# Three 256-column projection passes become one of 512 and one of 256, with the halves added by VectorE

## The chip, the cores and the metric

One core of one Trainium2 chip. The time is that of one execution of the whole program on the device, in microseconds (us); less is better. TensorE does the matrix products (a weight load and a matmul for each), ScalarE (ACT in the profile) the activations and conversions, VectorE (DVE) the elementwise arithmetic, and SyncE (SP) issues the transfers from HBM. A product leaves TensorE in a PSUM bank; the other two engines read it from there.

## The reference

The model is three layers over 256 tokens of width 1024. The change lies in the second half of the first layer, a mixture of 16,384 experts. Cut to what is computed there:

```python
u = expert_down[experts]                       # the chosen experts' input rows
act = gelu(einsum('cd,chkd->chk', xc, u))      # each expert's own projection of the token
w = gates * act
return einsum('chk,chkd->cd', w, expert_up[experts])
```

The kernel gathers nothing. It computes the projection of all 256 tokens on every expert, multiplies by a gate that is zero for an expert not chosen, and multiplies the result with all rows of `expert_up`.

## The kernel before

The experts are 128 chunks of 128. A chunk needs its projection (experts x tokens, from `peer_down`), the gelu of it, the gate, and then the product of these weights with the chunk's 128 x 1024 block of `peer_up`, added up over all chunks in four PSUM banks, `experts_acc`.

Products are made exact enough by splitting each fp32 operand into a high part that TensorE's fp32r format holds and a low part, what is left. `three_passes` then does high x high, high x low and low x high into the same PSUM columns (lines 187, 188, 189).

The projections of the first 52 chunks (`READY` is 28 + 24) are done earlier, in plain fp32. Those of the other 76, chunks 52 to 127, are the business of `Projections` and `experts_phase`. `hT` is the activation in its high and low part, each 8 slices (`k`) of 128 x 256 tokens. For chunk n:

- SP loads `down_raw` (in two halves) and then `ffn_h`, the raw rows of `peer_up`, in one queue.
- ACT writes `down_high`, DVE `down_low` (`split_high`, `split_low`, two halves each).
- TensorE does 8 x three passes of 256 columns into the left half of the bank `projection0` or `projection1`.
- ACT applies the gelu from that bank into `experts_full`, of which there is one; DVE multiplies it by the gate (`spread`), and writes its high and low part, `experts_wh` and `experts_wl`.
- ACT and DVE split the rows of `peer_up` into `experts_uh` and `experts_ul`; TensorE does 4 x three passes of 512 columns into `experts_acc`.

Every engine runs its own instructions in the written order and waits on semaphores. On TensorE the projection of chunk n + 1 stands ahead of the sum of chunk n:

```python
def both(n, b):
    proj.project(pe, n + 1, 1 - b)
    add(n, b)
```

ACT's order in a round is `split_high(n + 1)`, gelu of n, split of the rows n. DVE's is `split_low(n + 1)`, the gate of n, the weights of n, the low part of the rows n. The first two rounds and the last two are written out, the rest is a loop of two rounds.

Of the kernel before, what the change touches and what calls it, by code (L numbers as in the profile page):

```python
# [30 lines left out]
P = 128  # L31
# [1114 lines left out]
class Projections:  # L1146
# [3 lines left out]
    def __init__(self, nc, ctx, down, hT, raw):  # L1150
        self.down, self.hT, self.raw = down, hT, raw
        self.high, self.low = [[ctx.enter_context(nc.sbuf_tensor(f"down_{n}{b}", [P, KD, P], F32R)) for b in range(2)]
                               for n in ("high", "low")]
        self.u = [ctx.enter_context(nc.psum_tensor(f"projection{b}", [P, 512], F32)) for b in range(2)]
        self.landed = [[ctx.enter_context(nc.semaphore(f"down_landed{b}_{h}")) for h in range(2)] for b in range(2)]
        self.highs, self.lows, self.projected, self.done = [
            ctx.enter_context(nc.semaphore(n)) for n in ("down_highs", "down_lows", "projected", "gelu_done")]
# [25 lines left out]
    def project(self, pe, n, b):  # L1183
        m = n - READY
        for h in range(2):
            pe.wait_ge(self.lows, m * 2 + (h + 1))
            if h == 0:
                wait(pe, self.done, m - 1)
            for k in range(KD // 2 * h, KD // 2 * (h + 1)):
                mm = three_passes(pe, self.u[b][:, 0:SEQ], [v[b][:, k, :] for v in (self.high, self.low)],  # L1190
                                  [v[:, k, :] for v in self.hT], k == 0, k == KD - 1)
            mm.then_inc(self.projected, 1)

    def gelu(self, act, n, b, into):
        m = n - READY
        act.wait_ge(self.projected, m * 2 + 2)
        act.activation(into, self.u[b][:, 0:SEQ], ACT.Gelu).then_inc(self.done, 1)  # L1197
# [289 lines left out]
def experts_phase(nc, up, early, spread, x, proj, spare):  # L1487


    with ExitStack() as c:  # L1490
# [56 lines left out]
        def _(act):  # L1547
# [6 lines left out]
            def one(n, b):  # L1554
                if not isinstance(n, int) or n + 1 < NKEYS:
                    proj.split_high(act, n + 1, 1 - b)
                wait(act, wgt_ready, n)
                proj.gelu(act, n, b, full[:])
# [11 lines left out]
        def _(dve):  # L1570
# [10 lines left out]
            def one(n, b):  # L1581
                if not isinstance(n, int) or n + 1 < NKEYS:
# [4 lines left out]
                weights(n, b, full[:])  # L1587
            over_chunks(dve, 0, EARLY, lambda n, b: weights(n, b, early[:, n, :]))
            proj.split_low(dve, READY, 0)
            over_chunks(dve, EARLY, READY, lambda n, b: weights(n, b, early[:, n, :]))  # L1590
            for b in range(2):
                one(READY + b, b)
# [29 lines left out]
def build(nc, d, out, upto=99, start=0):  # L1622
    ctx = ExitStack()
    with ctx:
# [7 lines left out]
        hT = [sb(f"hT_{n}", [P, KD, SEQ], F32R) for n in ("high", "low")]  # L1632
# [37 lines left out]
        if start < 2 <= upto:  # L1670
            with ExitStack() as c:
# [18 lines left out]
                proj = Projections(nc, c, d["downT"], hT, plain.raw)  # L1690
# [71 lines left out]
```

## Time and profile before

| | before |
|---|---|
| three runs | 1721.66, 1725.54, 1726.55 us, median 1725.54 |
| profiled execution | 1728.26 us, of which 1726.2 us are the span of its instructions |
| TensorE busy in the span | 1564.6 us (91%) |
| VectorE busy | 1074.9 us (62%) |
| ScalarE busy | 699.1 us (40%) |
| mean granted TensorE clock | 0.955 of full speed |

Matmul records overlap: one of 256 columns shows a duration of 0.28 us where the next starts 0.12 us later. What a pass costs in a full row of passes is the distance from one start to the next. "Idle" in brackets behind a row is the time that the engine sat before it, and whose work ended that.

### The profile page before, as it was taken

Reading aid. Unit: us, or ns where it says so; the run is one execution under the profiler, and the core shown is the slowest. Engines: PE = TensorE matmul, PEld = TensorE weight load, DVE = VectorE, ACT = ScalarE, POOL = GpSimd, SP = SyncE. Lnnn points to the kernel's source line nnn. Section 1 sums busy time; section 2 is a strip of 40 time slices with the busy share of each in tenths; the row PEclk is TensorE's granted clock in tenths of the full one; section 3 lists DMA queues with packets and bytes.
Section 4 is the critical chain, followed back from the end, with each engine's and each line's share of the span. In section 5 each row is a group of like instructions: output and inputs, shape, how many; then the busy total and the mean of one; then the engine's idle time right before and its main releaser. Section 6 shows DMA issues by size and latency. Waiting matters only on the chain. (4 is left out here: it accounts for less than half of the span.)

```text
span 1726.2 us, 28966 instructions
## 1 busy us (share of the span) xinstructions
PE 1564.6 (91%) x8809; PEld 1383.0 (80%) x8809; DVE 1074.9 (62%) x2752; ACT 699.1 (40%) x1526; POOL 5.8 (0%) x13
## 2 busy tenths in 40 slices
PE   2997789998998999999999999879999997869987
PEld 1664578887997888999999999779999997658885
DVE  3577457957997776666666666555555554266663
ACT  0343211113323443544444444346555554336552
POOL 0000000000000000000000000000000000000000
PEclk9998789999999999999999999989999999679997
DMA  6410043442224555555555555374444441075410
GB/s 246 164 38 1 2 160 111 153 153 75 92 90 142 194 191 188 194 184 182 194 184 182 194 184 183 127 261 135 151 152 137 134 139 45 1 250 165 121 26 25
DMA packets 162586, 239.33 MB, mean 139 GB/s; under 512 B 41808, under 2 KB 91472, under 8 KB 161488
## 3 DMA queue, kind: packets, MB, share of 16 engines
q1 hardware_dynamic: 162160, 238.34, 42.2%
q8 instruction: 37, 0.61, 0.2%
q14 instruction: 37, 0.30, 0.1%
q10 hardware_dynamic: 352, 0.07, 0.0%
HBM read 237.09 MB, written 1.28 MB: 138 GB/s over the span
## 5 line engine op out<-in xcount | busy, mean ns | idle before, releaser
L187 PE MATMUL experts_acc<-experts_uh,experts_wh 128*128 128x512 f32 x512 | 201.5, 394 | 5.7 <-DVE experts_ul L1579 5.7
L188 PE MATMUL experts_acc<-experts_ul,experts_wh 128*128 128x512 f32 x512 | 201.1, 393 | 0.0
L189 PE MATMUL experts_acc<-experts_uh,experts_wl 128*128 128x512 f32 x512 | 200.1, 391 | 0.0
L1132 PE MATMUL plain_u<-ffn_h,down_raw 128*128 128x256 f32 x832 | 192.1, 382 | 0.4 <-PEq L1217 0.4
L1552 ACT ACTIVATE experts_uh<-ffn_h 128x512 fp32r<-128x512 f32 x256 | 147.1, 624 | 83.7 <-PE experts_acc L189 79.1
L189 PE MATMUL projection<-hT_high,down_low 128*128 128x256 f32 x608 | 172.1, 283 | 0.0
L188 PE MATMUL projection<-hT_low,down_high 128*128 128x256 f32 x608 | 172.0, 283 | 0.0
L187 PE MATMUL projection<-hT_high,down_high 128*128 128x256 f32 x608 | 171.7, 282 | 0.0
L1132 PEld LDWEIGHTS plain_u<-ffn_h,down_raw 128*128 128x128 f32 x832 | 154.1, 192 | 19.5 <-issue 1.1
L1579 DVE TENSOR_TENSOR experts_ul<-ffn_h,experts_uh 128x512 fp32r<-128x512 f32 x256 | 164.7, 684 | 3.0 <-ACT experts_uh L1552 3.0
L187 PE MATMUL mix_a_pj<-mix_a_wh,hT_high 128*128 128x384 f32 x384 | 136.8, 356 | 17.0 <-DVE mix_a_wl L560 17.0
L188 PE MATMUL mix_a_pj<-mix_a_wl,hT_high 128*128 128x384 f32 x384 | 130.1, 339 | 0.0
L189 PE MATMUL mix_a_pj<-mix_a_wh,hT_low 128*128 128x384 f32 x384 | 130.0, 339 | 0.0
L1585 DVE TENSOR_TENSOR experts_full<-experts_full,spread 128x256 f32<-128x256 f32 x76 | 32.3, 426 | 143.1 <-ACT experts_full L1197 143.1
L187 PEld LDWEIGHTS projection<-hT_high,down_high 128*128 128x128 f32 x608 | 116.4, 191 | 2.9
L188 PEld LDWEIGHTS projection<-hT_low,down_high 128*128 128x128 f32 x608 | 116.4, 191 | 2.9
L187 PEld LDWEIGHTS experts_acc<-experts_uh,experts_wh 128*128 128x128 f32 x512 | 97.1, 190 | 24.4 <-issue 6.1
L189 PEld LDWEIGHTS projection<-hT_high,down_low 128*128 128x128 f32 x608 | 116.4, 191 | 0.0
L189 PEld LDWEIGHTS experts_acc<-experts_uh,experts_wl 128*128 128x128 f32 x512 | 96.7, 189 | 20.8
L1173 ACT ACTIVATE down_high<-down_raw 128x512 fp32r<-128x512 f32 x152 | 95.0, 632 | 40.9 <-DMA down_raw<-in_downT 34.8
L188 PEld LDWEIGHTS experts_acc<-experts_ul,experts_wh 128*128 128x128 f32 x512 | 97.1, 190 | 17.4
L560 DVE TENSOR_TENSOR mix_a_wl<-mix_a_w_raw,mix_a_wh 128x1536 fp32r<-128x1536 f32 (+1 forms) x64 | 93.6, 1489 | 19.5 <-ACT mix_a_wh L710 16.3
(274 smaller groups left out, 3014.9 us busy)
## 6 DMA issues: line engine op xcount, KB each, us to landing
down_raw<-in_downT SPq DMA_DIRECT2D x256, 256.0 KB, 3.4
ffn_h<-in_up SPq DMA_DIRECT2D x256, 256.0 KB, 2.8
mix_a_w_raw<-in_wa SPq DMA_DIRECT2D x48, 768.0 KB, 5.9
block_w_raw<-in_w SPq DMA_DIRECT2D x16, 768.0 KB, 6.6
mix_b_w_raw<-in_wb SPq DMA_DIRECT2D x16, 768.0 KB, 6.7
route_raw<-in_route SPq DMA_DIRECT2D x16, 576.0 KB, 3.7
wo<-in_wo SPq DMA_DIRECT2D x2, 2048.0 KB, 10.4
mix_a_w_raw<-in_wa SPq DMA_DIRECT2D x16, 256.0 KB, 3.3
```

The lines of the kernel that those rows point to most:

```text
L187: pe.matmul(out, lhs[0], rhs[0], start=start, stop=False, skip_group_check=True)
L188: pe.matmul(out, lhs[0], rhs[1], start=False, stop=False, skip_group_check=True)
L189: return pe.matmul(out, lhs[1], rhs[0], start=False, stop=stop, skip_group_check=True)
L560: eng.tensor_tensor(wl[w][:, k, c], pieces.raw[w][:, k, c], wh[w][:, k, c].bitcast(F32), ALU.subtract).then_inc(lows, 1)
L1132: mm = pe.matmul(self.u[b][:, 0:SEQ], self.raw[b][:, k, :], self.h[:, k, :], start=k == 0, stop=k == KD - 1, skip_group_check=True)
L1173: act.activation(self.high[b][:, self.half(h)], self.raw[b][:, self.half(h)], ACT.Copy).then_inc(self.highs, 1)
L1552: act.activation(uh[b][:, w], raw_u[b][:, w], ACT.Copy).then_inc(u_high, 1)
L1579: dve.tensor_tensor(ul[b][:, w], raw_u[b][:, w], uh[b][:, w].bitcast(F32), ALU.subtract).then_inc(u_low, 1)
L1585: dve.tensor_tensor(full[:], full[:], spread[:, n - READY, :], ALU.mult)
```

## The change

The two activation parts become one tensor, `hT_both`, so that one matmul can read slice k of both: 256 columns of the high part and 256 of the low part, 8 KB apart. With the high weights loaded once, it writes high x high to the left half of the bank and high x low to the right half. The low weights then meet the high activations as before, into the left half. VectorE adds the halves into `experts_full` (a copy of one, a drain, an addition of the other), and ScalarE applies the gelu there in place. The semaphore `summed` now releases the gelu and the bank. The new step of VectorE for chunk n + 1 stands at the end of its round n, and for the first chunk right before the first round.

```diff
     def project(self, pe, n, b):
         m = n - READY
+        u = self.u[b][:]
         for h in range(2):
             pe.wait_ge(self.lows, m * 2 + (h + 1))
             if h == 0:
-                wait(pe, self.done, m - 1)
+                wait(pe, self.summed, m - 1)
             for k in range(KD // 2 * h, KD // 2 * (h + 1)):
-                mm = three_passes(pe, self.u[b][:, 0:SEQ], [v[b][:, k, :] for v in (self.high, self.low)],
-                                  [v[:, k, :] for v in self.hT], k == 0, k == KD - 1)
+                pe.matmul(u.rearrange("p (a t) -> p a t", a=2), self.high[b][:, k, :], self.hT[:, :, k, :], start=k == 0, stop=False,
+                          skip_group_check=True)
+                mm = pe.matmul(u[:, 0:SEQ], self.low[b][:, k, :], self.hT[:, 0, k, :], start=False, stop=k == KD - 1,
+                               skip_group_check=True)
             mm.then_inc(self.projected, 1)
 
-    def gelu(self, act, n, b, into):
+    def sum_halves(self, dve, n, b, into):
+
         m = n - READY
-        act.wait_ge(self.projected, m * 2 + 2)
-        act.activation(into, self.u[b][:, 0:SEQ], ACT.Gelu).then_inc(self.done, 1)
+        dve.wait_ge(self.projected, m * 2 + 2)
+        dve.tensor_copy(into, self.u[b][:, 0:SEQ])
+        dve.drain()
+        dve.tensor_tensor(into, into, self.u[b][:, SEQ:], ALU.add).then_inc(self.summed, 1)
+
+    def gelu(self, act, n, v):
+        m = n - READY
+        act.wait_ge(self.summed, m + 1)
+        act.activation(v, v, ACT.Gelu).then_inc(self.done, 1)
...
                 proj.split_high(act, n + 1, 1 - b)
-                wait(act, wgt_ready, n)
-                proj.gelu(act, n, b, full[:])
+                proj.gelu(act, n, full[:])
...
             def one(n, b):
-                if not isinstance(n, int) or n + 1 < NKEYS:
+                more = not isinstance(n, int) or n + 1 < NKEYS
+                if more:
                     proj.split_low(dve, n + 1, 1 - b)
                 dve.wait_ge(proj.done, n - (READY - 1))
                 dve.tensor_tensor(full[:], full[:], spread[:, n - READY, :], ALU.mult)
                 dve.drain()
                 weights(n, b, full[:])
+                if more:
+                    dve.drain()
+                    proj.sum_halves(dve, n + 1, 1 - b, full[:])
...
+            proj.sum_halves(dve, READY, 0, full[:])
             for b in range(2):
                 one(READY + b, b)
...
-        hT = [sb(f"hT_{n}", [P, KD, SEQ], F32R) for n in ("high", "low")]
+        hT_both = sb("hT", [P, 2, KD, SEQ], F32R)
+        hT = [hT_both[:, n] for n in range(2)]
```

On VectorE, where the first two rounds begin, before (after the loop over the ready chunks):

```order
L1206 COMPARE_AND_BRANCH
L1180 TENSOR_TENSOR down_low<-down_raw,down_high 128x512 x2
L1585 TENSOR_TENSOR experts_full<-experts_full,spread 128x256
L1574 CAST experts_wh<-experts_full 128x256
L1576 TENSOR_TENSOR experts_wl<-experts_full,experts_wh 128x256
L1579 TENSOR_TENSOR experts_ul<-ffn_h,experts_uh 128x512 x2
```

The same place now:

```order
L1217 COMPARE_AND_BRANCH
L1201 COPY experts_full<-projection 128x256
L1203 TENSOR_TENSOR experts_full<-experts_full,projection 128x256
L1180 TENSOR_TENSOR down_low<-down_raw,down_high 128x512 x2
L1596 TENSOR_TENSOR experts_full<-experts_full,spread 128x256
L1584 CAST experts_wh<-experts_full 128x256
L1586 TENSOR_TENSOR experts_wl<-experts_full,experts_wh 128x256
L1589 TENSOR_TENSOR experts_ul<-ffn_h,experts_uh 128x512 x2
L1201 COPY experts_full<-projection 128x256
L1203 TENSOR_TENSOR experts_full<-experts_full,projection 128x256
```

Two instructions that read the finished projection (`projection`) have come in ahead of the next chunk's low weights (`down_low`), at the start and in each round.

On TensorE, the end of a loop's sum and the first products of the next projection, before:

```order
L189 MATMUL experts_acc<-experts_uh,experts_wl 128x512
L1206 REGISTER_ALU
L1206 COMPARE_AND_BRANCH
L187 MATMUL projection<-hT_high,down_high 128x256
L188 MATMUL projection<-hT_low,down_high 128x256
L189 MATMUL projection<-hT_high,down_low 128x256
```

A piece of a projection now, inside the loop:

```order
L1187 ISA
L1191 MATMUL projection<-hT,down_high 128x512
L1193 MATMUL projection<-hT,down_low 128x256
L1191 MATMUL projection<-hT,down_high 128x512
L1193 MATMUL projection<-hT,down_low 128x256
```

Three matmuls for a slice k, of 768 columns together, have become two, of 768 columns together.

## Rows read from the trace of the kernel before

**Rows 1.** Stretch, length, busy us (xinstructions) of PE, PEld, DVE, ACT, POOL; PEclk, DMA, GB/s.
```profile
692.62:1108.50 415.88, 415.88 (x2666) 379.55 (x2665) 263.62 (x519) 196.94 (x368) 0.00 (x0) 1.00 0.56 185
```

**Rows 2.** Waits, 692.62 to 1108.50 us: engine line <- releaser, us, times, longest.
```profile
ACT experts_full L1197 <- PE projection L189: 174.2, 73, 2.9
DVE experts_full L1585 <- ACT experts_full L1197: 134.5, 72, 1.9
```

**Rows 3.** Timeline of TensorE: start us, us, engine line op.
```profile
692.62 0.40 PE L187 MATMUL experts_acc<-experts_uh,experts_wh 128*128 128x512 f32 x1
...
1002.65 0.39 PE L188 MATMUL experts_acc<-experts_ul,experts_wh 128*128 128x512 f32 x1
...
1004.24 0.39 PE L189 MATMUL experts_acc<-experts_uh,experts_wl 128*128 128x512 f32 x1
1004.47 0.28 PE L187 MATMUL projection<-hT_high,down_high 128*128 128x256 f32 x1
1004.58 0.28 PE L188 MATMUL projection<-hT_low,down_high 128*128 128x256 f32 x1
...
1007.22 0.28 PE L189 MATMUL projection<-hT_high,down_low 128*128 128x256 f32 x1
1007.34 0.40 PE L187 MATMUL experts_acc<-experts_uh,experts_wh 128*128 128x512 f32 x1
```

**Rows 4.** Timeline of TensorE in the next layer, passes of 384 columns.
```profile
1251.78 0.34 PE L187 MATMUL mix_a_pj<-mix_a_wh,hT_high 128*128 128x384 f32 x1
...
1255.25 0.34 PE L189 MATMUL mix_a_pj<-mix_a_wh,hT_low 128*128 128x384 f32 x1
```

**Rows 5.** Timeline of VectorE, its first two rounds.
```profile
683.67 1.28 DVE L1180 TENSOR_TENSOR down_low<-down_raw,down_high 128x512 fp32r<-128x512 f32 x2
690.42 0.43 DVE L1585 TENSOR_TENSOR experts_full<-experts_full,spread 128x256 f32<-128x256 f32 x1 [5.47 <-ACT experts_full L1197]
690.92 0.29 DVE L1574 CAST experts_wh<-experts_full 128x256 fp32r<-128x256 f32 x1
691.29 0.43 DVE L1576 TENSOR_TENSOR experts_wl<-experts_full,experts_wh 128x256 fp32r<-128x256 f32 x1
691.63 1.29 DVE L1579 TENSOR_TENSOR experts_ul<-ffn_h,experts_uh 128x512 fp32r<-128x512 f32 x2
692.84 1.28 DVE L1180 TENSOR_TENSOR down_low<-down_raw,down_high 128x512 fp32r<-128x512 f32 x2
694.04 0.42 DVE L1585 TENSOR_TENSOR experts_full<-experts_full,spread 128x256 f32<-128x256 f32 x1
```

**Rows 6.** VectorE instructions that read PSUM, by group.
```profile
L1439 DVE COPY spread_i<-slots 128x256 f32<-128x256 f32 x2 | 0.8, 420 | 1.0 <-PEq L1217 1.0
L890 DVE TENSOR_TENSOR mix_a_ona<-mix_a_ot,mix_a_inv 128x256 f32<-128x256 f32 x8 | 3.4, 425 | 3.8 <-PE mix_a_ot L662 2.9
```

**Rows 7.** Timeline of ScalarE, the last rounds.
```profile
1099.09 1.31 ACT L1173 ACTIVATE down_high<-down_raw 128x512 fp32r<-128x512 f32 x2 [0.21 <-DMA down_raw<-in_downT]
1108.76 0.39 ACT L1197 ACTIVATE experts_full<-projection 128x256 f32<-128x256 f32 x1 [4.20 <-PE projection L189]
```

**Rows 8.** Timeline of SyncE's queue.
```profile
1004.47 0.93 SPq L1511 DMA_DIRECT2D ffn_h<-in_up  x2
1005.70 0.92 SPq L1163 DMA_DIRECT2D down_raw<-in_downT  x2
```

**Rows 9.** Timeline of TensorE at the second projection and at the last chunks.
```profile
689.74 0.28 PE L187 MATMUL projection<-hT_high,down_high 128*128 128x256 f32 x1
...
1108.50 0.40 PE L187 MATMUL experts_acc<-experts_uh,experts_wh 128*128 128x512 f32 x1
...
1111.25 0.45 PE L187 MATMUL experts_acc<-experts_uh,experts_wh 128*128 128x512 f32 x1
```

**Rows 10.** Timeline of VectorE, the last round.
```profile
1109.18 0.42 DVE L1585 TENSOR_TENSOR experts_full<-experts_full,spread 128x256 f32<-128x256 f32 x1 [3.13 <-ACT experts_full L1197]
1110.39 1.29 DVE L1579 TENSOR_TENSOR experts_ul<-ffn_h,experts_uh 128x512 fp32r<-128x512 f32 x2
```

More of the change, by code:

```diff
@@ L1155, in __init__ @@
         self.landed = [[ctx.enter_context(nc.semaphore(f"down_landed{b}_{h}")) for h in range(2)] for b in range(2)]
-        self.highs, self.lows, self.projected, self.done = [
-            ctx.enter_context(nc.semaphore(n)) for n in ("down_highs", "down_lows", "projected", "gelu_done")]
+        self.highs, self.lows, self.projected, self.summed, self.done = [
+            ctx.enter_context(nc.semaphore(n)) for n in ("down_highs", "down_lows", "projected", "halves_summed", "gelu_done")]
     def load(self, sp, n, b):
@@ L1689, in build @@
                 c1.close()
-                proj = Projections(nc, c, d["downT"], hT, plain.raw)
+                proj = Projections(nc, c, d["downT"], hT_both, plain.raw)
                 experts_phase(nc, d["up"], early, spread, x, proj, plain.h)
```

## The prediction

> **What bounds the kernel now.** I read the busy time of the experts' own stretch first, then its waits, then the timeline of each engine around one round. From the first sum after two projections (692.62 us) to the last but one sum (1108.50) TensorE is busy for all of 415.88 us, at full clock; VectorE for 263.62, ScalarE for 196.94 [rows 1]. That is the proof to look for, and since overlapping matmuls make "busy" flatter TensorE, the waits are the second one: the long waits are ScalarE's for the projection (174.2 us) and VectorE's for the gelu behind it (134.5 us), and TensorE waits for nobody [rows 2]. So in this stretch the end is set by how fast TensorE can start its passes, 74 rounds of 415.88 / 74 = 5.62 us [rows 1, 3]. The round has two parts: the projection, 1004.47 to 1007.34, 2.87 us for 24 passes of 256 columns, and the sum, the other 2.75 us, 12 passes of 512 [rows 3]. The change touches only this stretch of 76 projections and both its ends.
>
> **What a pass costs.** Seven steps from 1002.65 to 1004.24 make 227 ns for a pass of 512 columns, and with the first passes of a sum in, 2.75 / 12 gives 229; I take 228. From 1004.58 to 1007.22 are 22 steps of 256 columns: 120 ns [rows 3]. Passes of 384 columns, 20 steps from 1251.78 to 1255.25, take 173.5 ns [rows 4]. The three lie on one line: 120, 174, 228, that is 54 ns for each 128 columns and 12 ns that every pass pays whatever its width.
>
> **The change on TensorE.** A slice k now has 3 passes of 256, 3 x 120 = 360 ns. Afterwards it has one of 512 and one of 256, 228 + 120 = 348 ns. The number of columns is the same; what goes is one fixed part of 12 ns. Over 8 slices that is 0.096 us in a round, 5.52 in place of 5.62, and over 76 projections (608 slices) 7.3 us.
>
> What the rows don't show is a pass whose 512 columns come from two places 8 KB apart, and passes of two widths in turn. The dear end: the two runs cost what two passes cost, 240 ns, and nothing is saved. The cheap end: the first step of a projection, from a 256 pass that stands behind a 512 one, is 1004.47 to 1004.58, 0.11 us, not 0.12 [rows 3]; if every narrow pass had that, a slice would take 228 + 113 = 341 ns at the best reading of it, and 608 x 19 = 11.6 us would go. A step into the sum, 512 behind 256, shows nothing of such a gain, so I take the value of the long runs, 348.
>
> The Trainium skill ("TensorE: Matmul & The Clock Gate", section "Back-to-back issue gap") gives a warm pass N / 2.4 GHz plus about 2.5 ns, so that a pass less would be worth 2.5 ns and the change 608 x 2.5 = 1.5 us. The trace has 120 ns where that formula has 109, and 228 where it has 216: here the fixed part is some 12 ns, and I go by the trace.
>
> **The change on VectorE, and what hides it.** Each round gets a copy from PSUM, a drain, an addition, and a drain ahead of them. A copy of 128x256 from PSUM takes 0.42 us, an elementwise operation of two operands with one in PSUM 0.425 [rows 6]. Such an instruction, a drain and the next start are 690.42 to 690.92, 0.50 us, and one without a drain ahead of the next 691.29 to 691.63, 0.34 [rows 5]. The first drain is at most the difference, 0.16. A round of VectorE that waits for nothing is 690.42 to 694.04, 3.62 us [rows 5]; it becomes 3.62 + 0.50 + 0.34 + 0.16 = 4.62. TensorE's is 5.52, so VectorE still waits each round, about 0.9 us less what the hand-over costs.
>
> What is queued behind the new wait is the point to check. Let Q be the moment when a projection is through and TensorE begins the sum. ScalarE started on it at Q + 0.26 (1108.50 to 1108.76) [rows 7, 9]; now VectorE does. Copy and addition: the next chunk's low weights start at Q + 0.26 + 0.84 = Q + 1.10 and their first half (1.28 - 0.60 = 0.68 us) is there at Q + 1.8. Before they were made well ahead. TensorE wants them when its sum is through, at Q + 2.75: 1 us to spare. The gelu ends near Q + 1.6, ahead of the low weights' end at Q + 2.3. Then gate 0.50, cast 0.37, subtraction 0.34, first half of the rows' low part 0.68: Q + 4.2, wanted by the sum at Q + 2.75 + 2.78 = Q + 5.5: 1.3 us to spare. SyncE's queue loads the next rows when that low part is done, and the expert weights behind them: before at 1004.47 and 1005.70 [rows 8], which are 2.75 and 3.98 us behind Q = 1001.72 (one round of 5.62 before 1007.34). The first moves to Q + 4.2, 1.5 us later, and the weights with it. ScalarE waited for them until 1099.09, 1.83 us behind its Q of 1108.50 - 2 x 5.62 = 1097.26 [rows 7, 9], so they land at Q + 3.4 now and are converted by Q + 4.7; VectorE takes them at Q + 5.52 + 1.10 = Q + 6.6. All of it is covered. If the cover were gone, each 0.1 us of a round would cost 7.6 us. ScalarE's work is the same; the gelu reads `experts_full` in place of PSUM.
>
> **The two ends, which have no cover.** At the start the low weights of the second projection were made at 683.67, long before, and TensorE went from the first projection into the second at 689.74 without a gap [rows 5, 9]. Now they stand behind the first addition: 689.74 + 0.26 + 0.84 + 0.68 = 691.52. TensorE idles 1.8 us. What follows holds: the rows' low part is there at 691.52 - 0.68 + 1.20 + 1.21 + 0.68 = 693.9, the second projection ends at 691.52 + 2.78 = 694.3. At the end the last sum starts at 1111.25 [rows 9], its rows' first low half being there at 1110.39 + 0.68 = 1111.07 [rows 10], 0.18 us before. Copy, drain and addition push the gelu from Q + 0.26 to Q + 0.26 + 0.50 + 0.43 + 0.04, 0.97 later. The last sum loses 0.97 - 0.18 = 0.8 us. Together 2.6 us.
>
> **The sum.** - 7.3 + 2.6 = - 4.7 us. Made against the profiled execution, 1728.26, it gives 1723.5. That execution lies 2.7 above the median 1725.54 of the three runs, so on the scale of the runs the forecast is 1720.8, 0.27% less. A measurement of this kernel can tell about 0.3% (5.2 us) from no change: the forecast lies just inside that.
>
> **The rivals.**
> A. Nothing is saved on TensorE: the pass that reads two places costs 240 ns. For it speaks that no pass of this trace reads so; against it, that the fixed part is the same at three widths. The time is the two ends alone, + 2.6: 1728.1. (By the formula of the Trainium skill cited above it would be - 1.5 + 2.6 = + 1.1, so 1726.6, between A and the forecast; its page would have A nearly right.)
> B. The narrow pass behind a wide one is cheaper, 341 ns for a slice: - 11.6 + 2.6 = - 9.0, 1716.5. For it speaks the one step of 0.11 us; against it that it occurs once in 24.
> C. Slower: VectorE becomes the bound. Its round of 4.62 and the hand-over of 0.26 make 4.9 us; it decides once the copy, the two drains and the addition cost 0.6 us more than I give them, since the round would then pass 5.52. At a round of 5.8 us the stretch takes 76 x 0.18 = 14 us more than before and the ends 2.6: 1742. Against it: all durations are from rows of the same engine on the same shapes.
>
> **How the numbers follow.** Forecast 0.60, A 0.20, B 0.12, C 0.08. The forecast's own spread is some 3 us to either side, from the runs (1721.66 to 1726.55) and the ends: 1718 to 1724. The range reaches from B, 1716, to A, 1728; C is left out. The forecast falls below 1720.3, that is faster by over 0.3%, in a little under half of its cases (0.27), with B 0.39 in all. Slower by over 0.3% are C and a little of A: 0.09. The rest, 0.52, is within 0.3%.
>
> **What would show it.** In the changed profile: a step from a wide projection pass to the narrow one of 228 ns and back of 120, rounds of 5.52 us, TensorE busy throughout; VectorE waiting for the projection in each round, by 0.6 to 0.9 us; the low weights' first half done 1 us ahead of the projection; one gap on TensorE of 1.8 us ahead of the second projection and one of 0.8 ahead of the last sum. Rounds of 5.62 mean A, of 5.47 B. TensorE waiting for `down_low` or `experts_ul` in every round means C. Wrong it would also be if the clock fell in one of the two gaps, which are short.

## The result, and the profile after

The changed kernel takes 1725.9 us (median of 17 runs, 1723.99 to 1728.99), the kernel before 1717.47 in the runs beside it. The ratio is 1.0045, 95% interval [1.0035, 1.0056]: slower by 0.45%. The forecast was 4.7 us less than before, 1720.8. The profiled execution of the changed kernel has a span of 1722.7 us at a mean clock of 0.959.

The view that splits the span into stretches shows where to look. Its columns are those of [rows 1]. For the changed kernel the cuts are the start of the first projection's first pass and the start of the experts' last pass:

```profile
0.00:686.15 686.15, 610.19 (x2937) 501.55 (x2938) 475.21 (x1492) 192.84 (x519) 1.40 (x7) 0.96 0.36 125
686.15:1113.72 427.57, 425.25 (x2129) 356.90 (x2127) 329.33 (x682) 203.80 (x376) 0.00 (x0) 1.00 0.54 181
1113.72:1722.70 608.98, 523.61 (x3138) 489.12 (x3136) 330.57 (x730) 305.02 (x631) 4.40 (x6) 0.93 0.40 125
```

and the same cuts in the execution profiled before the change was made:

```profile
0.00:686.87 686.87, 611.06 (x2937) 502.16 (x2938) 476.17 (x1494) 192.86 (x519) 1.40 (x7) 0.96 0.37 125
686.87:1113.83 426.96, 426.96 (x2736) 389.55 (x2735) 268.02 (x528) 200.83 (x376) 0.00 (x0) 1.00 0.55 182
1113.83:1726.20 612.37, 526.54 (x3138) 491.27 (x3136) 330.68 (x730) 305.43 (x631) 4.41 (x6) 0.92 0.40 124
```

The changed stage grew by 0.61 us, from 426.96 to 427.57, with a full clock in both. So two questions stand: why the stage didn't shrink by 4.7 us, and where the other 7 us or so of the runs come from. The stretch behind the stage can't answer the second from these two profiles: in the one of before it is the longer, and its clock the lower.

**The first question.** The stretch that answers to [rows 1], from the first sum after two projections to the last but one sum:

```profile
693.62:1107.49 413.87, 413.87 (x2075) 347.79 (x2073) 321.90 (x667) 199.83 (x368) 0.00 (x0) 1.00 0.56 186
```

It is 413.87 / 74 = 5.593 us a round, where the forecast had 5.52 and before had 5.62. The timeline of TensorE in one round (columns as in [rows 3]):

```profile
1001.21 0.40 PE L187 MATMUL experts_acc<-experts_uh,experts_wh 128*128 128x512 f32 x1
1001.46 0.40 PE L188 MATMUL experts_acc<-experts_ul,experts_wh 128*128 128x512 f32 x1
1001.69 0.40 PE L189 MATMUL experts_acc<-experts_uh,experts_wl 128*128 128x512 f32 x1
...
1004.00 0.39 PE L1191 MATMUL projection<-hT,down_high 128*128 128x512 f32 x1
1004.22 0.28 PE L1193 MATMUL projection<-hT,down_low 128*128 128x256 f32 x1
1004.34 0.40 PE L1191 MATMUL projection<-hT,down_high 128*128 128x512 f32 x1
1004.57 0.28 PE L1193 MATMUL projection<-hT,down_low 128*128 128x256 f32 x1
1004.69 0.40 PE L1191 MATMUL projection<-hT,down_high 128*128 128x512 f32 x1
1004.93 0.28 PE L1193 MATMUL projection<-hT,down_low 128*128 128x256 f32 x1
1005.05 0.40 PE L1191 MATMUL projection<-hT,down_high 128*128 128x512 f32 x1
...
1006.81 0.40 PE L187 MATMUL experts_acc<-experts_uh,experts_wh 128*128 128x512 f32 x1
```

The projection is 1004.00 to 1006.81, 2.81 us or 351 ns a slice, forecast 348. The sum is 1001.21 to 1004.00, 2.79 us where it was 2.75; its first step, 1001.21 to 1001.46, is the longest. Both parts are longer than forecast though nobody is waited for. Over 71 rounds a wide pass is followed after 227 to 241 ns, 235 on average, and the narrow one behind it after 113 to 120, 116 on average. So the narrow pass behind a wide one is cheaper, as rival B had it, and the wide one behind a narrow one is dearer by more than that.

The two ends came as forecast. TensorE's timeline at the second projection and at the last sum:

```profile
688.84 0.28 PE L1193 MATMUL projection<-hT,down_low 128*128 128x256 f32 x1
690.74 0.49 PE L1191 MATMUL projection<-hT,down_high 128*128 128x512 f32 x1 [1.61 <-DVE down_low L1180]
...
1110.04 0.39 PE L189 MATMUL experts_acc<-experts_uh,experts_wl 128*128 128x512 f32 x1
1111.13 0.47 PE L187 MATMUL experts_acc<-experts_uh,experts_wh 128*128 128x512 f32 x1 [0.70 <-DVE experts_ul L1589]
```

A pass of 256 is followed by the next after 0.12 us, here after 1.90: 1.78 lost. A pass of 512 is followed after 0.23, here after 1.09: 0.86 lost.

VectorE's waits are what [rows 2] become (686 to 1108 us):

```profile
ACT experts_full L1208 <- DVE experts_full L1203: 134.5, 75, 7.0
ACT down_high L1173 <- DMA down_raw<-in_downT: 79.7, 73, 1.5
DVE experts_full L1201 <- PE projection L1193: 74.6, 75, 6.1
PE projection L1191 <- DVE down_low L1180: 1.6, 1, 1.6
```

VectorE waits for the projection in each of 75 rounds, 6.1 us ahead of the first and (74.6 - 6.1) / 74 = 0.93 in the others; TensorE waits once for VectorE here. ScalarE's wait for the expert weights is the later transfer that the forecast worked out, and nobody waits for it in turn.

### The profile page after: what moved, and what is told of

Its sections match the earlier page's. It is cut to its first block and busy times, and to the rows that moved or that the text cites. A ratio compares the mean times of both kernels' runs of the same rounds, so it can differ in the third digit from the quotient of the medians.

```text
span 1722.7 us, 27941 instructions
## 1 busy us (share of the span) xinstructions
PE 1559.1 (90%) x8201; PEld 1347.6 (78%) x8201; DVE 1135.1 (66%) x2904; ACT 701.7 (41%) x1526; POOL 5.8 (0%) x13
## 5 line engine op out<-in xcount | busy, mean ns | idle before, releaser
L1191 PE MATMUL projection<-hT,down_high 128*128 128x512 f32 x608 | 217.1, 397 | 1.6 <-DVE down_low L1180 1.6
L1193 PE MATMUL projection<-hT,down_low 128*128 128x256 f32 x608 | 170.5, 280 | 0.0
L187 PE MATMUL mix_a_pj<-mix_a_wh,hT 128*128 128x384 f32 x384 | 136.6, 356 | 16.2 <-DVE mix_a_wl L560 16.2
L1191 PEld LDWEIGHTS projection<-hT,down_high 128*128 128x128 f32 x608 | 114.2, 188 | 29.2 <-DVE down_low L1180 1.9
L189 PE MATMUL mix_a_pj<-mix_a_wh,hT 128*128 128x384 f32 x384 | 130.0, 338 | 0.0
L188 PE MATMUL mix_a_pj<-mix_a_wl,hT 128*128 128x384 f32 x384 | 129.9, 338 | 0.0
L1193 PEld LDWEIGHTS projection<-hT,down_low 128*128 128x128 f32 x608 | 114.7, 189 | 2.9
L189 PEld LDWEIGHTS experts_acc<-experts_uh,experts_wl 128*128 128x128 f32 x512 | 96.6, 189 | 22.9
L560 DVE TENSOR_TENSOR mix_a_wl<-mix_a_w_raw,mix_a_wh 128x1536 fp32r<-128x1536 f32 (+1 forms) x64 | 93.8, 1489 | 19.9 <-ACT mix_a_wh L710 16.6
L1180 DVE TENSOR_TENSOR down_low<-down_raw,down_high 128x512 fp32r<-128x512 f32 x152 | 98.1, 686 | 4.5 <-issue 0.3
L597 PE MATMUL block_pj<-block_w_raw,block_h 128*128 128x384 f32 x256 | 91.1, 487 | 1.1 <-PEq L206 1.1
L1208 ACT ACTIVATE experts_full<-experts_full 128x256 f32<-128x256 f32 x76 | 31.8, 418 | 138.6 <-DVE experts_full L1203 138.6
```

Of the source, the lines that this page charges most:

```text
L187: pe.matmul(out, lhs[0], rhs[0], start=start, stop=False, skip_group_check=True)
L188: pe.matmul(out, lhs[0], rhs[1], start=False, stop=False, skip_group_check=True)
L189: return pe.matmul(out, lhs[1], rhs[0], start=False, stop=stop, skip_group_check=True)
L560: eng.tensor_tensor(wl[w][:, k, c], pieces.raw[w][:, k, c], wh[w][:, k, c].bitcast(F32), ALU.subtract).then_inc(lows, 1)
L597: mm = pe.matmul(dst[:, 0:3 * P], hT[:, k, chunks[i][1] * P:(chunks[i][1] + 1) * P], pieces.raw[b][:, k, :], start=k == 0, stop=k == KD - ...
L1180: eng.tensor_tensor(self.low[b][:, k], self.raw[b][:, k], self.high[b][:, k].bitcast(F32), ALU.subtract).then_inc(self.lows, 1)
```

## The experiments

All were timed beside the kernel before on the same chip. "Stage" is the distance between the two cuts above in the kernel's own profile; the last column is the median of the mean granted clocks of its runs. In the runs of before beside them it was 0.963 or 0.964, in those of the changed kernel 0.959 and, the second time, 0.957.

| kernel | median us | ratio [95%] | stage | clock |
|---|---|---|---|---|
| before_again | 1720.93 | 1.0000 [0.9981, 1.0019] | 426.96 | 0.964 |
| after_again | 1728.95 | 1.0041 [1.0024, 1.0059] | 427.64 | 0.957 |
| one_run | 1726.72 | 1.0034 [1.0017, 1.0052] | 427.56 | 0.959 |
| early_low | 1722.11 | 1.0007 [0.9989, 1.0024] | 426.68 | 0.962 |
| before_late | 1719.69 | 0.9999 [0.9986, 1.0012] | 426.97 | 0.964 |
| after_late | 1723.62 | 1.0017 [1.0002, 1.0031] | 427.64 | 0.962 |
| grouped | 1725.37 | 1.0021 [1.0007, 1.0034] | 424.17 | 0.958 |
| narrow_sum | 1726.94 | 1.0034 [1.0023, 1.0046] | 429.77 | 0.961 |
| after_060 | 1726.05 | 1.0048 [1.0035, 1.0062] | 427.61 | 0.960 |
| before_300 | 1720.59 | 1.0015 [1.0005, 1.0025] | 426.93 | 0.963 |
| before_341 | 1719.20 | 1.0010 [0.9999, 1.0021] | 426.96 | 0.964 |
| wide_first | 1721.26 | 1.0017 [1.0006, 1.0027] | 421.36 | 0.960 |
| after_padded | 1722.27 | 1.0031 [1.0020, 1.0042] | 427.58 | 0.964 |
| before_padded | 1723.93 | 1.0037 [1.0023, 1.0051] | 426.93 | 0.962 |
| wide_first_padded | 1716.52 | 0.9990 [0.9977, 1.0002] | 421.37 | 0.963 |
| after_free | 1721.88 | 1.0005 [0.9994, 1.0016] | 427.65 | 0.961 |
| wide_first_free | 1714.32 | 0.9964 [0.9951, 0.9977] | 421.36 | 0.963 |
| before_free | 1720.81 | 1.0024 [1.0015, 1.0033] | 426.96 | 0.961 |

### Is the difference there again, and where

The kernel before and the changed kernel, run again as they are.

> The kernel before, unchanged, for a second profile. The changed stage (first projection to the last sum) took 436.2 us in the profile of before and 436.8 after, while the medians lie 8.4 us apart. Theory T1: the stage is as in the first profile, 436.2 us within 0.3, and the rest of the program is some 9 us shorter than in that profile, because TensorE is granted the low clock for fewer microseconds in the layers behind the stage (it was low for 154 us in the first profile, 140 after); mean clock 0.96 or above. Theory T2: the stage itself is some 8 us shorter than in the first profile (428), which was an odd execution, and the rest is as it was.

> The changed kernel, unchanged. Both theories: a stage of 436.8 us within 0.3, a ratio of 1.003 to 1.006 to before. T1: the later layers take as long as in the first profile of it; T2 says nothing of them.

(The stages of 436.2 and 436.8 us in these texts run on to the next norm's transposes; the cuts of the table end 9.2 us earlier.) The difference came again, 1.0041, and so did the stages, 426.96 and 427.64. The kernel before now showed this stretch behind the stage:

```profile
1115.00:1717.10 602.10, 516.41 (x3138) 482.41 (x3136) 330.89 (x730) 305.33 (x631) 4.41 (x6) 0.95 0.41 126
```

602.10 us at a clock of 0.95, against 612.37 at 0.92 in its first profile: the same instructions, 10 us apart from one execution to the next. In the changed kernel it was 608.98 and 610.0. So what the change costs beside 0.6 us lies behind the changed code, in the two layers that the diff doesn't touch, and single profiles can't be set against each other there.

### The stage: does the pass pay for its two places

The activation as `[slice, part, token]`, so that a wide pass reads one run of 512 columns (the matmuls, cut here, index it to match).

```diff
-        hT_both = sb("hT", [P, 2, KD, SEQ], F32R)
-        hT = [hT_both[:, n] for n in range(2)]
+        hT_both = sb("hT", [P, KD, 2, SEQ], F32R)
+        hT = [hT_both[:, :, n, :] for n in range(2)]
...
```

> The changed kernel with the high and low activations of a slice side by side, so that the wide pass reads one run of 512 columns and not two of 256 that lie 8 KB apart. In the changed kernel a wide projection pass is followed after 227 to 241 ns, mean 235, where 228 were forecast. Theory R (the second run costs time): the step falls to 228, a projection from 2.81 to 2.75 us, the stage by 75 x 0.06 = 4.5 us. Theory S (it is the alternation of wide and narrow passes, whatever is read): steps, round and stage as in the changed kernel, within 0.5 us of the stage. The whole may move differently by the clock of the later layers, if T1 holds.

Projection 2.8101 us, sum 2.7832, stage 427.56: as in the changed kernel. Two places cost nothing. What rival A was built on isn't there.

### The stage: the changes of width

Four wide passes, then four narrow ones, in each half.

```diff
-            for k in range(KD // 2 * h, KD // 2 * (h + 1)):
+            part = range(KD // 2 * h, KD // 2 * (h + 1))
+            for k in part:
                 pe.matmul(u.rearrange("p (a t) -> p a t", a=2), self.high[b][:, k, :], self.hT[:, :, k, :], ...
+            for k in part:
                 mm = pe.matmul(u[:, 0:SEQ], self.low[b][:, k, :], self.hT[:, 0, k, :], ...
```

> The changed kernel, with the passes of a half of a projection grouped: four wide ones, then four narrow ones, in place of wide and narrow in turn. In the changed kernel a projection takes 2.810 us (2.784 forecast) and the sum behind it 2.783 (2.748 before). If it is the change of width that costs (theory S), there are 3 changes in a projection and not 15: projection 2.79 us, sum back near 2.75, round 5.54, stage shorter by 75 x 0.05 = 4 us. If the sum's passes are slow because a wide pass stands right before, or because VectorE reads the bank in that time, nothing changes there.

And all eight wide passes first, which need only the high weights; the low weights' wait then stands behind them. The wide pass and the wait for `summed` go out of the loop (lines cut here).

```diff
+        pe.wait_ge(self.highs, m * 2 + 2)
+        wait(pe, self.summed, m - 1)
+        for k in range(KD):
+            pe.matmul(u.rearrange("p (a t) -> p a t", a=2), self.high[b][:, k, :], self.hT[:, :, k, :], ...
         for h in range(2):
             pe.wait_ge(self.lows, m * 2 + (h + 1))
...
```

> The changed kernel with all eight wide passes of a projection ahead of all eight narrow ones; the wide ones wait only for the high weights, so that TensorE has 1.8 us of work while VectorE makes the low weights of the second projection. In the grouped kernel (three changes of width) projection and sum took 2.780 and 2.767 us, in the changed one (fifteen) 2.810 and 2.783, and with narrow passes alone 2.873 and 2.747. Theory S: with one change of width 2.77 and 2.76, round 5.53 against 5.62 before and 5.593 changed; the gap of 1.85 us goes; stage 426.96 - 75 x 0.09 + 0.9 = 421.1 us, 5.9 below before. Rival: the slow passes behind a wide one cost the same wherever they stand, round 5.55 as grouped, stage 422.6. The whole: 1720 - 5.9 plus what the clock does, 0 to 8.

The projection took 2.780 us with four groups and 2.766 with two; the sum 2.767 and 2.7475, the latter its length of before. The stage fell to 424.17 and 421.36, 3.4 and 6.2 us below the changed kernel's where 4 and 6.5 were expected. The whole did not follow: 1.0021 and 1.0017, still slower than before though the stages are 2.8 and 5.6 us shorter than there. One round with two groups (timeline of TensorE in wide_first_free, whose stage is the same; a row with x8 is eight passes):

```profile
1002.01 1.98 PE L1191 MATMUL projection<-hT,down_high 128*128 128x512 f32 x8
1003.82 1.11 PE L1196 MATMUL projection<-hT,down_low 128*128 128x256 f32 x8
1004.78 0.40 PE L187 MATMUL experts_acc<-experts_uh,experts_wh 128*128 128x512 f32 x1
1005.01 0.40 PE L188 MATMUL experts_acc<-experts_ul,experts_wh 128*128 128x512 f32 x1
```

Eight wide passes in 1.81 us, 226 ns each; eight narrow ones in 0.96, 120 each. That is the 346 ns a slice that the forecast's fixed part asks for (348). Removing a pass does save 13 ns: (2.872 - 2.766) / 8. Fifteen changes of width in a projection, in place of one, give back 5 ns a slice and slow the sum behind it by 36 ns. Two groups leave a gap at the start, but it has moved to the first sum, whose rows' low part is the last thing that VectorE makes there:

```profile
695.96 0.47 PE L187 MATMUL experts_acc<-experts_uh,experts_wh 128*128 128x512 f32 x1 [1.15 <-DVE experts_ul L1594]
```

The first two projections and this gap take 688.92 to 695.96, 7.04 us, where the changed kernel takes 686.15 to 693.62, 7.47.

### The stage: do VectorE's reads of PSUM slow TensorE

High x high and high x low as two passes of 256 again, into the two halves, with VectorE adding as in the changed kernel.

```diff
-                pe.matmul(u.rearrange("p (a t) -> p a t", a=2), self.high[b][:, k, :], self.hT[:, :, k, :], start=k == 0, ...
+                pe.matmul(u[:, 0:SEQ], self.high[b][:, k, :], self.hT[:, 0, k, :], start=k == 0, stop=False, ...
+                pe.matmul(u[:, SEQ:], self.high[b][:, k, :], self.hT[:, 1, k, :], start=False, stop=False, ...
```

> The changed kernel, but the wide pass is two passes of 256 again, high x low into the right half of the bank; VectorE still adds the halves. It does only that half of the change. If the passes of TensorE make the sum slower (theory S), projection 2.872 and sum 2.748 us as before, round 5.62, stage 427 + 1.85 + 0.9 = 429.7 us. If VectorE's two new reads of PSUM beside the sum make it slower (theory V), the sum is 2.783.

Projection 2.8726 and sum 2.7473, both as before. VectorE's copies and additions cost TensorE nothing in a round. The stage is 429.77, which is before's plus 2.8: the two ends alone, and what rival A would have been.

### The stage: the gap at the start

The low weights of the second projection ahead of the first addition (in the first round they are then left out; that line is cut here).

```diff
...
+            proj.split_low(dve, READY + 1, 1)
             proj.sum_halves(dve, READY, 0, full[:])
```

> The changed kernel, but VectorE makes the low weights of the second projection before it adds the halves of the first. The gap of 1.85 us on TensorE ahead of the second projection goes, and nothing else in the stage changes: stage 436.8 - 1.8 = 435.0 us, 1.2 below before. If the stage decided the whole (T2), the whole is 1.8 us shorter than the changed kernel. T1: the whole moves by 1.8 or by another amount, since the stage now ends 1.8 us earlier against the windows of the clock.

The stage lost 0.96 us, not 1.8, and the timeline says why: the gap has moved to the first sum, whose rows' low part is late now.

```profile
693.81 0.47 PE L187 MATMUL experts_acc<-experts_uh,experts_wh 128*128 128x512 f32 x1 [0.66 <-DVE experts_ul L1589]
```

### Behind the stage: is it the moment at which the layers begin

The layers behind the stage have stretches at a granted clock below 1, and a shift in time could place them otherwise. These kernels delay them by idle subtractions of VectorE behind the last sum (results unused): before_late by 0.6 us, before_300 by 3.06, before_341 by 3.46; after_060 by 0.6 and after_late by 2.8. T1 and T1b in the texts below say that the moment at which the later layers begin decides the whole; T0 and the plain theory say that it doesn't. The lines are those of before_300.

```diff
+            for i in range(4):
+                dve.tensor_tensor(ul[0][:, halves[0]], raw_u[0][:, halves[0]], uh[0][:, halves[0]].bitcast(F32), ALU.subtract)
+                dve.drain()
```

> The kernel before, with one idle subtraction of 128x512 on VectorE (0.60 to 0.68 us) between the last sum and what follows it. It puts the end of the stage where the changed kernel has it, 0.6 us later than before, and changes nothing else. Clock theory T1 (the windows in which the low clock is granted lie fixed against the stage, which starts after such a window, and the small shift of its end decides how many windows of the later layers are at the low clock): the whole is 5 to 9 us slower than before, mean clock 0.959 or less, as the changed kernel. Plain theory: it costs its 0.65 us, ratio 1.000 to 1.001.

> The changed kernel, with 2.8 us of idle subtractions on VectorE between the last sum and what follows it. [...] T1: the later layers meet the windows as in before, so the whole is that of before plus some 3.4 us, 1723.6, and FASTER than the changed kernel (1728.9 in the last comparison) although it does 2.8 us more. Plain theory: 2.8 us slower than the changed kernel.

> The changed kernel with 0.6 us of idle work on VectorE between the last sum and what follows. [...] Theory T1b, that this shift decides: here it is +0.2, so 0 or -1, and the whole is 1720.1 + 0.65 + 0.6 - 0.5 = 1721, some 7 us FASTER than the changed kernel though it does 0.6 us more. Theory T0, that the changed program makes the later layers slower by itself: 0.6 slower than the changed kernel, 1727 to 1729.5.

> The kernel before with 3.06 us of idle work at the same place. [...] T1b: + 3.06 + 8 = 11 us slower than before, about 1731, ratio 1.006. T0: + 3.06, ratio 1.0018.

> [...] T1b: +3.44, about 1723.6, ratio 1.002, and so faster by 7 us than the one with 3.06 us. T0: 0.4 us slower than that one.

No delay made the kernel before as slow as the changed one: 0.9999, 1.0015 and 1.0010, and 3.06 and 3.46 us of added work are 0.18% and 0.20%. after_060 stayed at 1.0048. Only after_late fits the theory: with 2.8 us more to do it ran at 1.0017. One in five isn't a cause, and I dropped it for the difference as a whole, though the moment plays a part in after_late that I can't name.

### Behind the stage: where TensorE's code lies

Then I set the later layers of all profiles side by side. One wait differed in every kernel with the changed TensorE program and in none with the length of before (narrow_sum included). It is VectorE's, for the bias tile, behind the last norm: 9.1 to 9.8 us there, 6.7 to 7.5 in the others. For before_again, beginning with the last norm's transposes (`norm_pt`):

```profile
1517.86 3.68 PE L243 MATMUL norm_pt<-ident,norm_h 128*128 128x128 f32 x16 [5.88 <-DVE norm_h L254]
...
1538.22 0.56 DVE L819 TENSOR_TENSOR bias_btile<-bias_braw,near 128x384 f32<-128x384 f32 x1 [7.09 <-DMA bias_braw<-bias_pad]
...
1543.94 0.66 PE L623 MATMUL mix_b_xp<-ident,mix_b_qk 128*128 128x128 f32 x4 [2.20 <-DVE mix_b_qk L813]
```

and for the changed kernel:

```profile
1519.42 3.68 PE L243 MATMUL norm_pt<-ident,norm_h 128*128 128x128 f32 x16 [5.87 <-DVE norm_h L254]
...
1542.21 0.56 DVE L819 TENSOR_TENSOR bias_btile<-bias_braw,near 128x384 f32<-128x384 f32 x1 [9.51 <-DMA bias_braw<-bias_pad]
...
1548.28 1.12 PE L623 MATMUL mix_b_xp<-ident,mix_b_qk 128*128 128x128 f32 x4 [4.97 <-DVE mix_b_qk L813]
```

From the transposes to the tile are 20.36 us in the one and 22.79 in the other, 2.4 more; to TensorE's `mix_b_xp` it is 2.8 more. The other 0.36 us goes with the change on VectorE: from the tile to `mix_b_xp` are 6.1 us in every kernel that adds the halves, narrow_sum too, and 5.7 in those that don't. The view of the transfers has a queue of the kind "instruction" (packets, MB, share); I take its packets for pieces of an engine's own program. In the changed kernel one lands between 1534 and 1536 us, in the middle of the transfer waited for:

```profile
q1 hardware_dynamic: 55, 0.90, 106.5%
q8 instruction: 1, 0.02, 3.0%
```

It is so in all profiles: the eight kernels with the short TensorE program have such a piece of 16 KB between the transposes and the tile, and the twelve others, the later ones with drains among them, have none. But early_low and after_late are among the eight, with waits of 9.2 and 9.1 us and ratios of 1.0007 and 1.0017, so this wait alone doesn't make a kernel slow.

The six written-out projections of the changed kernel have 8 matmuls and 8 weight loads less each. So all code of TensorE behind the stage lies 96 instructions nearer to its start, and by theory F its pieces are fetched at other moments. To test it, 96 drains on TensorE put the code back. First all of them stood behind the last sum:

```diff
             add(NKEYS - 1, 1, stop=True)
+            for _ in range(96):
+                pe.drain()
```

> The changed kernel with 96 drains on TensorE behind the last sum of the experts, where TensorE waits some 9 us anyway. The changed kernel has 96 instructions fewer on TensorE ahead of the later layers than the kernel before (six written-out projections, each with 8 matmuls and 8 weight loads less), so its later code lies 96 instructions nearer to the start; the drains put it back. Theory F (what costs 8 us behind the stage is where TensorE's code lies, since its blocks of code are fetched at other moments): bias_btile starts 17 us behind the last norm_pt matmul instead of 19 to 20, the first mix_b_xp matmul 22.5 to 23.2 behind it instead of 25.2 to 25.9, the mix_a products take 321 us instead of 320, and the whole comes to that of the kernel before plus the stage's 0.65: ratio 1.000 to 1.001. Rival K (the clock or VectorE's program decides, not TensorE's code): bias_btile stays at 19 to 20, ratio 1.004 to 1.005.

> The kernel before with the same 96 drains in the same place, so that its later code lies 96 instructions further from the start than anywhere so far. Theory F: the fetches of TensorE's code in the later layers come earlier in the program's work than in the kernel before, and some of the later steps move: mix_a products above 321 us, or bias_btile at another distance from the last norm_pt than 17 us; in which direction the total goes it does not say. Rival K: nothing behind the stage changes, bias_btile at 16.8 to 17.5, ratio 1.000 within 0.1%.

> Eight wide passes, then eight narrow ones (as in wide_first), with the 96 drains behind the last sum. Its stage was 5.6 us shorter than before's, yet the whole 1.0017. Theory F: with the later code where the kernel before has it, the layers behind take what they take there, so the whole comes to 1720 - 5.6 = 1714.5, ratio 0.996 to 0.997, faster than both kernels. Rival K: it stays at 1.0017.

The later layers came back as theory F said: in after_padded `bias_btile` starts 16.8 us behind the last transpose (19.1 to 19.9 in the unpadded ones), `mix_b_xp` 22.9, mix_a's products take 321.0 us. But the drains took time, some 0.07 us each (an estimate, since no view shows them: from the end of the last sum's last pass to the next norm's first step are 8.3 us, of which 1.4 pass after the last engine is through, as in the changed kernel, and 6.9 / 96 = 0.07), and a barrier of all engines stands behind them, so that the way from the last sum to mix_a's first product grew from 19.3 to 23.7 us. With this 4.4 taken off, the ratios of 1.0031 and 0.9990 would be 1.0005 and 0.9964. The totals that I had put down for after_padded and wide_first_padded failed by this cost. before_padded came out as neither theory had it: theory F named products above 321 us or a moved tile, and they took 319.3 us with the tile at 17.0; rival K named no change within 0.1%, and without the drains' time (here 4.5 us) it is 1.0011.

So in the next three 28 drains stood there and 68 ahead of the transposes of the norm behind it, where TensorE waits 8.8 us in all.

> The changed kernel with the 96 drains where they hold nobody up: 28 behind the last sum of the experts, 68 ahead of the next norm's transposes, each 0.068 us. In after_padded all 96 stood ahead of a barrier and made the stretch from the last sum to mix_a's products 4.4 us longer; taken off, it was 0.2 us above the kernel before. Theory F: that stretch takes 19.3 us again, mix_a's products 321 us, bias_btile 17 us behind the last norm_pt, and the whole is the kernel before plus 0.65 us: ratio 1.000 to 1.001. Rival K (the later layers took their time back only because the drains delayed them): 1.004 or more.

> Eight wide passes, then eight narrow ones, with the drains placed as in after_free. Theory F: the whole is the kernel before less the 5.6 us of the stage: ratio 0.9965 to 0.9975, faster than both. Rival K: 1.001 or more, as in wide_first.

> The kernel before with the same drains in the same two places as in after_free. It asks whether the drains in themselves, and not the position of the code behind them, made after_free quicker by 0.4%. Theory F: the drains give nothing by themselves; the kernel before is moved 96 instructions away from its position and gets 0 to 0.2% slower (before_padded, less the 4.4 us that its drains cost, was 1.9 us slower): ratio 1.000 to 1.002. Rival D (drains in TensorE's idle time keep it, or its clock, in a better state): ratio 0.995 to 0.997, as much below the kernel before as after_free is below the changed kernel.

after_free: 1.0005, where the changed kernel has 1.0045, and 1.0041 on the chip of this run; its interval meets neither of theirs. Its stage is the changed kernel's, 427.65 us, slow steps and gaps and all. wide_first_free: 0.9964 [0.9951, 0.9977], faster than both kernels. In before_free the same drains made the kernel slower, 1.0024, so drains as such give nothing (rival D); it is 0.04% above the range that I gave theory F. There the drains move the code away from where it was. The timeline of after_free:

```profile
1519.50 3.68 PE L245 MATMUL norm_pt<-ident,norm_h 128*128 128x128 f32 x16 [5.88 <-DVE norm_h L256]
...
1539.78 0.56 DVE L821 TENSOR_TENSOR bias_btile<-bias_braw,near 128x384 f32<-128x384 f32 x1 [7.00 <-DMA bias_braw<-bias_pad]
...
1545.86 0.66 PE L625 MATMUL mix_b_xp<-ident,mix_b_qk 128*128 128x128 f32 x4 [2.44 <-DVE mix_b_qk L815]
```

20.28 us from the transposes to the tile. Between 1520 and 1545 us no piece of code is fetched in it; one is between 1514 and 1516, when the transfers have hardly begun.

The products of the layer ahead, mix_a, move as well, with the code in before's place (before_again, after_free) and out of it (before_free, the changed kernel). In the order before_again, before_free, changed kernel, after_free (duration in ns least/median/most, then the first and the last start in us):

```profile
L187 PE MATMUL mix_a_pj<-mix_a_wh,hT_high x384: 334/334/686, 1134.3 to 1454.6; 128*128 128x384 f32 x192
```
```profile
L187 PE MATMUL mix_a_pj<-mix_a_wh,hT_high x384: 334/334/689, 1132.2 to 1451.4; 128*128 128x384 f32 x192
```
```profile
L187 PE MATMUL mix_a_pj<-mix_a_wh,hT x384: 334/334/689, 1133.0 to 1452.5; 128*128 128x384 f32 x192
```
```profile
L187 PE MATMUL mix_a_pj<-mix_a_wh,hT x384: 333/334/687, 1133.4 to 1454.7; 128*128 128x384 f32 x192
```

320.3, 319.2, 319.5 and 321.3 us: here the moved code is 1 to 2 us quicker. Moved code isn't slower everywhere; its place is worth a microsecond or two here, with the other sign than at the bias tile.

What is left of every ratio when its own stage and its added idle time are taken off says how far theory F carries. Put back by drains (four kernels): -0.03 to +0.02%. With before's length: -0.10 to 0% in four, but +0.18% in narrow_sum. Short, as in the changed kernel: +0.30 to +0.50% in six of eight, but +0.09% in early_low and -0.03% in after_late. Longer than before: +0.11% in before_padded, +0.23% in before_free.

## Why the prediction was wrong

**What bounds the kernel, and the two ends: right.** TensorE sets the stage's end in both kernels, VectorE waits 0.93 us a round (forecast 0.6 to 0.9), no rival C. The gaps were forecast at 1.8 and 0.8 us and measured 1.78 and 0.86.

**The change on TensorE: right in kind, too large by 5.3 us.** The term was -7.3 us. It measured (5.593 - 5.620) x 75 = -2.0. The fixed part of a pass is there, wide_first shows 13 ns for a pass less. What the term left out is the price of passes of two widths in turn: 351 ns a slice for 348, and above all 36 ns on the sum behind the projection, whose passes the change doesn't touch. Rival B's gain, a narrow pass of 0.11 us for 0.12 behind a wide one, is there (116 ns on average). What I missed is its counterpart, the price of a wide pass behind a narrow one: in the trace of before the first five passes of a sum are followed after 228 to 236 ns, the others after 226 or 227 (means over 70 rounds), and I had put that into one average of 228. Half of the missing 0.07 us a round lies outside the changed instructions, where the working had no term at all.

**The sum: the step that failed.** It was - 7.3 + 2.6, made against the profiled execution, with everything behind the last sum taken to be as before ("The change touches only this stretch of 76 projections and both its ends"). Of the 12.4 us between the forecast ratio (-4.7 us) and the measured one (0.0045 x 1717 = +7.7), the stage has 5.3 (-2.0 + 2.6 = +0.6 in place of -4.7). The greater part, 7.7 - 0.6 = 7 us, came from the two layers behind, whose instructions are the same. after_free shows the cause as far as the 96 missing instructions: with TensorE's code back in its place and nothing else mended, the ratio is 1.0005, and 0.6 us of stage are 1.0004; before_free shows that drains alone don't help. VectorE's program is longer too, and no run puts that back, but after_free has it as the changed kernel has. Of how these 7 us are made up, 2.4 are seen in the rows, the wait for the bias tile, with a fetch of code in the midst of its transfer in the slow case and none in the quick one. That the fetch is what delays the transfer is argued from this, not tried apart. The rest goes with the clock: the runs of the changed kernel had a median clock of 0.959, those of before 0.963 or 0.964, of after_free 0.961. An estimate: 0.005 of the mean over 1720 us is 17 us more at 1.2 GHz in place of 2.4, which costs up to 8.6 us where TensorE sets the time. Why later layers whose steps move by a microsecond or two get a lower clock stays open. So do early_low and after_late, whose code lies as in the changed kernel, with the same fetch in the same wait, and whose 1.0007 and 1.0017 (2.8 us of it added work) are better than theory F has it, and narrow_sum, at 1.0034 with before's code position, of which its stage explains 1.0016.

**How the numbers follow.** That 1725.9 us still lies between A and B is luck, since the scale was off as well. The forecast stood on a profile 1728.26 us long, and the chance for "slower by over 0.3%" (0.09) came from rivals within the stage alone. The 17 runs of before beside the changed kernel have a median of 1717.47, 8 us below the three runs that I had. No rival was that a part of the program which isn't touched could move by more than the whole effect forecast, though [rows 1] and the profile's clock line were only ever read for the stage.

**The rule of the Trainium skill.** The rows of TensorE's steps showed a fixed part of 12 ns, and wide_first gave 13 ns for each pass removed. The Trainium skill ("TensorE: Matmul & The Clock Gate", section "Back-to-back issue gap") has N / 2.4 GHz plus 2.5 ns, but for a pass by itself, a condition that the forecast left out. For a stream of weight loads and matmuls it has about 131 ns at 512 columns. The trace agrees with neither: 227 ns a pass of 512 in long runs. By the 2.5 ns the total would have come out nearer to the truth (1726.6, an estimate from that page's figure), for a reason that isn't the right one.

## What to carry to other kernels

Fewer, wider passes pay far better when passes of the same width stand together: here one pass less a slice gave 2.0 us over the rounds with widths in turn and 8.0 with one change of width. Cost the change of width and the passes behind it, not only the pass removed, and put those first that wait for least. When an edit changes the number of instructions written out on TensorE, everything behind it moves in the program and can change by several microseconds with not an instruction altered; try the edit with the removed count filled up in idle time before believing a difference of half a percent, of either sign. Compare layers that you don't touch over several profiles of each kernel, since one and the same kernel showed 602 and 612 us for them.

## What the runs showed of the hardware that was not expected

- Passes of 512 and 256 columns in turn take 351 ns a pair, in groups of eight 346, and the 12 passes of 512 behind the alternating ones take 2.783 us in place of 2.747.
- A wide pass that reads two runs of 256 columns 8 KB apart is as quick as one that reads 512 in one run (2.8100 and 2.8101 us a projection).
- 96 instructions more or less on TensorE, ahead of layers that stay the same, moved the whole by 0.4% (1.0045 and 1.0005), and in the kernel before by 0.24%.
- 96 drains on an idle TensorE, ahead of a point where all engines meet, cost 4.4 us; by the estimate above, one takes some 0.07 us.
